# A folded token Fourier transform in a one-core diffusion trunk kernel, with its steps interleaved over four bank sides

## What is computed

```python
def _fourier(f, w_f):
    B, L, _ = f.shape
    fg = f.reshape(B, L, FNET_GROUPS, FNET_GROUP_DIM).astype(jnp.float32)
    z = jnp.fft.fft2(fg, axes=(1, 3), norm='ortho').real.astype(f.dtype)
    return z.reshape(B, L, FNET_DIM) @ w_f
...
y = lax.conv_general_dilated(u, p['conv_w'][:, None, :].astype(u.dtype), window_strides=(1,),
                             padding=((CONV_WIDTH // 2, CONV_WIDTH // 2),),
                             dimension_numbers=('NWC', 'WIO', 'NWC'), feature_group_count=CONV_DIM)
```

## Time and profile before

| | |
|---|---|
| median of 3 runs | 1306.79 us (1306.72 to 1307.79) |
| the profiled execution | 1307.94 us, its span 1306.1 us |
| mean granted TensorE clock | 0.966 of 2.4 GHz |
| busy, PE / DVE / ACT / POOL | 93% / 69% / 47% / 24% of the span |
| Fourier stage on PE, first uv product to first v product | 159.7 to 210.0 us |
| attention on PE | 296.7 to 411.4 us |
| expert stage | from about 740 us on |

### The profile page before, as it was taken

How to read it: one execution, slowest core, us unless ns; L and a number is a source line. 1 busy time by engine, 2 the same in 40 slices (tenths; PEclk the granted TensorE clock), 3 DMA queues, 4 the chain that set the end, 5 groups by cost and what they waited for, 6 DMA issues and landing times.

```text
span 1306.1 us, 18927 instructions
## 1 busy us (share of the span) xinstructions
PE 1215.0 (93%) x7383; PEld 984.0 (75%) x7383; DVE 899.5 (69%) x1015; ACT 617.0 (47%) x686; POOL 311.3 (24%) x207
## 2 busy tenths in 40 slices
PE   4899879998999999999995399999999999999995
PEld 3798669998998999999995266666666666666663
DVE  3599766454553325523747489999999999999996
ACT  4311222224443124123213277777777777777774
POOL 1041100000443222323315202222222222222224
PEclk9899979999999989999997599999999999999998
DMA  9876642322111212244318999999999999999985
GB/s 321 266 205 208 200 93 65 100 78 73 50 50 65 65 33 65 80 162 146 100 44 314 333 346 368 381 379 380 380 379 380 381 381 381 380 381 381 386 312 179
DMA packets 156264, 302.89 MB, mean 232 GB/s; under 512 B 7058, under 2 KB 60821, under 8 KB 155952
## 3 DMA queue, kind: packets, MB, share of 16 engines
q1 hardware_dynamic: 145636, 272.80, 58.4%
q0 software_dynamic: 3872, 12.78, 4.3%
q10 hardware_dynamic: 6700, 16.51, 3.5%
HBM read 286.98 MB, written 15.08 MB: 231 GB/s over the span
## 4 chain that ended last, share of the span: by engine, by line
PE 86%; DVE 5%; DMA 3%; POOL 2%; ACT 1%; issue 1%; SPq 0%; ACTq 0%; POOLq 0%; DVEq 0%
PE bank L1500 17%; PE bank L1501 16%; PE bank L1502 16%; PE bank L1524 5%; PE bank L1526 5%; PE bank L1525 5%; PE bank L1528 5%; PE bank L1529 5%; PE bank L1527 5%; DMA wring<-in_w_ada 2%; PE bank L1752 2%; DVE fa L1060 1%; PE bank L1737 1%; PE bank L1805 1%; PE bank L1924 1%
## 5 line engine op out<-in xcount | busy, mean ns | idle before, releaser
L897 ACT CAST h2r_a<-w_a 128x2048 fp32r<-128x2048 f32 x96 | 183.7, 1914 | 84.8 <-PE bank L1502 77.0
L1500 PE MATMUL bank<-h2r_a,xTh 128*80 128x512 f32 x384 | 152.5, 397 | 1.0 <-DVE xTl L1417 1.0
L563 POOL TENSOR_TENSOR half<-half 1x1 f32<-1x1 f32 x33 | 69.7, 2112 | 351.3 <-DVE ye L1467 348.3
L1502 PE MATMUL bank<-h2r_a,xTl 128*80 128x512 f32 x384 | 150.5, 392 | 0.0
L493 POOL TENSOR_TENSOR lring<-wring,hring 128x2048 fp32r<-128x2048 f32 x21 | 99.1, 4719 | 178.5 <-ACT hring L631 178.5
L1501 PE MATMUL bank<-l2r_b,xTh 128*80 128x512 f32 x320 | 125.8, 393 | 0.0
L1411 DVE TENSOR_TENSOR l2r_b<-w_a,h2r_b 128x2048 fp32r<-128x2048 f32 x48 | 110.3, 2299 | 17.8 <-ACT h2r_b L897 17.8
L1411 DVE TENSOR_TENSOR l2r_b<-w_a,h2r_a 128x2048 fp32r<-128x2048 f32 x48 | 109.9, 2289 | 10.4 <-ACT h2r_a L897 10.4
L1411 DVE TENSOR_TENSOR l2r_a<-w_a,h2r_a 128x2048 fp32r<-128x2048 f32 x48 | 109.5, 2282 | 9.3 <-ACT h2r_a L897 7.7
L1060 DVE SCALAR_TENSOR_TENSOR fa<-fa,cwT 128x655 f32<-128x655 f32 x120 | 111.5, 972 | 1.4
L897 ACT CAST h2r_b<-w_a 128x2048 fp32r<-128x2048 f32 x48 | 91.9, 1914 | 34.7 <-PE bank L1502 31.9
(11 more groups left out here) (344 smaller groups left out, 3036.7 us busy)
## 6 DMA issues: line engine op xcount, KB each, us to landing
w_a<-in_w_e_gate SPq DMA_DIRECT2D x64, 1024.0 KB, 12.2
w_a<-in_w_e_up SPq DMA_DIRECT2D x64, 1024.0 KB, 13.0
w_b<-in_w_e_down SPq DMA_DIRECT2D x48, 1024.0 KB, 12.2
wring<-in_w_in SPq DMA_DIRECT2D x20, 1024.0 KB, 5.3
w_a<-in_w_e_down SPq DMA_DIRECT2D x16, 1024.0 KB, 13.1
fa<-in_w_ada SPq DMA_DIRECT2D x14, 1024.0 KB, 7.8
wring<-in_w_ada SPq DMA_DIRECT2D x10, 1024.0 KB, 9.2
fa<-in_w_in SPq DMA_DIRECT2D x4, 1024.0 KB, 11.2
```

What stands on the lines that cost most here:

```text
L897: act.copy(h2r[k % 3], w2[k]).then_inc(e_hi, 1)
L1500: pe.matmul(out, lh, rh, start=start, stop=False)
L1502: return pe.matmul(out, ll, rh, start=False, stop=stop)
```

## The change

The latent tokens of f are folded: with x the 512 tokens, even part x[t] + x[512 - t] and odd part x[t] - x[512 - t] for t = 1 to 255, and tokens 0 and 256 as they are. The cosine product then needs only the even part, and the sine product only the odd part; and only outputs 0 to 256 are made, from which the others follow by a sum and a difference (`fold_back`). ACT first copies f's latent part to a new tile `fs`, DVE folds it into `eo`, ACT and DVE split `eo`.

- uv(g) has 2 jobs in place of 5: 18 products (3 of 256 columns, 15 of 128, of which 3 for token 256 alone) in place of 15 of 256.
- z(g) has 21 products (9 of 260 columns, 6 of 256, 6 of 128) in place of 24 of 512 and 6 of 128. Of the 9, three are over one partition, for token 256.
- z jobs get bank sides of their own (4 and 5, 6 and 7), and PE's order becomes uv 0, uv 1, z 0, uv 2, z 1, uv 3, z 2, the first value tile, z 3, the other value tiles.
- The tables take one unit (dft 0, three DMAs, 0.5 MB) in place of two of 1 MB; unit in 8 takes the second's place, ahead of the last four ada units.
- `Vs`, from which the values are stored, lies in the tile `vw`. POOL's 8 bias DMAs wait also for ACT's high part of unit in 4.
- Convolution taps: 9 between the f blocks (before 20), 6 in the uv and z steps (18), 7 behind in 9, 6 behind each of in 4, 5, 6, 7, 20, 21, then one in each of the 20 attention iterations that copy an output, and the last 4 at the end of attention.

```diff
-UNITS += [("ada", 18), ("ada", 19), ("dft", 0), ("dft", 1)] + [("ada", i) for i in range(20, 24)]
-UNITS += [("in", i) for i in (8, 9, 4, 5, 6, 7)]
+UNITS += [("ada", 18), ("ada", 19), ("dft", 0), ("in", 8)] + [("ada", i) for i in range(20, 24)]
+UNITS += [("in", i) for i in (9, 4, 5, 6, 7)]
...
+HALF = NS // 2
+DFT_C, DFT_S, DFT_M = 0, 2 * (HALF + 4), 2 * (HALF + 4) + 2 * HALF
+DFT_N = DFT_M + HALF + 4
...
-JOBS += [("uv", 0, t) for t in range(TT)]
-for _g in range(4):
-    if _g < 3:
-        JOBS += [("uv", _g + 1, t) for t in range(TT)]
-    JOBS += [("z", _g)]
-JOBS += [("v", u, t) for u in range(2) for t in range(TT)]
+JOBS += [("uv", g, t) for g in range(2) for t in range(2)] + [("z", 0)]
+JOBS += [("uv", 2, 0), ("uv", 2, 1), ("z", 1), ("uv", 3, 0), ("uv", 3, 1), ("z", 2)]
+JOBS += [("v", 0, 0), ("z", 3)] + [("v", 0, t) for t in range(1, TT)] + [("v", 1, t) for t in range(TT)]
...
+    out, turn = [], 0
+    for j in JOBS:
+        if j == ("fnet", 0):
+            turn = 1
+        if j[0] == "z":
+            out.append(2 + j[1] % 2)
+        elif j[0] == "g2":
+            out.append(0)
+        else:
+            out.append(turn)
+            turn = 1 - turn
+    return out
+
+
+SIDE = sides()
+FIRST, SECOND = (0, 1, 4, 6), (2, 3, 5, 7)
...
-        Vs = xg_f[:, 0:2048].rearrange("p (t d) -> p t d", t=4)
+        Vs = vw[:, :, :, :].rearrange("p a b n -> p (a b) n")
...
+        fs = fa[:, 4608:5632].rearrange("p (b t) -> p b t", b=2)
+        eo = fa[:, 5632:6656].rearrange("p (b t) -> p b t", b=2)
+        qs = xg_f[:, 0:2560].rearrange("p (b t) -> p b t", b=2)[:, :, 1024:1280]
...
+                if UNITS[u][0] == "dft":
+                    x, n = raw(u), HALF + 4
+                    tab = consts["dft_l"]
+                    sp.dma_start(x[:, DFT_C:DFT_S].rearrange("p (c k) -> p c k", c=2), tab[0, :, 0:2, 0:n]).then_inc(s_w[SLOT[u]], 16)
+                    sp.dma_start(x[:, DFT_S:DFT_M].rearrange("p (c k) -> p c k", c=2),
+                                 tab[1, :, 0:2, 0:HALF]).then_inc(s_w[SLOT[u]], 16)
+                    sp.dma_start(x[0:1, DFT_M:DFT_N], tab[0, 0:1, 2, 0:n]).then_inc(s_w[SLOT[u]], 16)
+                    return
...
             gp.wait_ge(s_ada, 24)
+            gp.wait_ge(s_hi, SPLITS.index(U_OF[("in", 4)]) + 1)
             for r in range(8):
...
-                for t, b in job_halves(n):
-                    ins = act.copy(bh[:, i, t], b)
-                ins.then_inc(s_fh, 1)
+                (_, b0), (_, b1) = job_halves(n)
+                act.copy(bh[:, i, 0:NP], b0[:, 0:NP])
+                if i >= 2:
+                    act.wait_ge(s_eo, i - 1)
+                act.copy(fs[:, i % 2, 0:TH - NP], b0[:, NP:TH])
+                act.copy(fs[:, i % 2, TH - NP:NS], b1).then_inc(s_fh, 1)
+                act.wait_ge(s_eo, i + 1)
+                act.copy(bh[:, i, NP:T], eo[:, i % 2, :]).then_inc(s_fh, 1)
...
+                w, n = g % 2, J_OF[("uv", g, 0)]
+                act.wait_ge(s_job, n + 1)
+                act.copy(uvh[:, w, 0:512], bank_a(n)[:, :]).then_inc(s_uvh, 1)
+                n += 1
+                act.wait_ge(s_job, n + 1)
+                act.copy(uvh[:, w, 512:768], bank_a(n)[:, 0:256])
+                act.copy(uvh[0:1, w, 768:896], bank_a(n)[0:1, 256:384]).then_inc(s_uvh, 1)
...
+            def z_out(g):
                 n = J_OF[("z", g)]
                 act.wait_ge(s_job, n + 1)
-                bs, bp = job_bank(n)
-                act.copy(Z[:, g, NP:T], bs)
-                act.copy(Z[:, g, 0:NP], bp).then_inc(s_ja, 1)
-
-            hi(U_OF[("in", 9)])
+                zp, zq = bank_a(n), bank_b(n)
+                act.copy(Z[:, g, 0:NP], zq[:, 0:NP])
+                act.copy(Z[:, g, NP + HALF:NP + HALF + 1], zp[:, HALF:HALF + 1])
+                if g >= 2:
+                    act.wait_ge(s_jd, freed(J_OF[("z", g - 2)])[1])
+                act.copy(qs[:, g % 2, :], zq[:, NP:NP + HALF]).then_inc(s_zq, 1)
...
+            uv_hi(0)
+            uv_hi(1)
+            act.wait_ge(s_rpb2, 16)
+            z_out(0)
+            uv_hi(2)
+            z_out(1)
+            uv_hi(3)
+            z_out(2)
...
+            v_out(0, 0)
+            z_out(3)
+            hi(U_OF[("in", 9)])
+            v_out(0, 1)
+            hi(U_OF[("in", 4)])
...
-                ins.then_inc(s_jd, 1)
+                dve.wait_ge(s_fh, 2 * i + 1)
+                x, y, w = fs[:, i % 2, :], eo[:, i % 2, :], i % 2
+                dve.tensor_tensor(y[:, 1:HALF], x[:, 1:HALF], x[:, NS - 1:HALF:-1], ALU.add)
+                dve.tensor_tensor(y[:, HALF + 1:NS], x[:, 1:HALF], x[:, NS - 1:HALF:-1], ALU.subtract)
+                dve.tensor_copy(y[:, 0:NS:HALF], x[:, 0:NS:HALF]).then_inc(s_eo, 1)
+                dve.tensor_tensor(bl[:, i, 0:NP], bank_a(n)[:, 0:NP], bh[:, i, 0:NP].bitcast(F32), ALU.subtract).then_inc(s_jd, 1)
                 rows_out(16 + 2 * i)
                 ada_mod(15 + 2 * i)
...
-                if i in (1, 2):
-                    lo(U_OF[("dft", i - 1)])
-                conv(4 if i in (1, 2) else 6)
+                if i == 1:
+                    lo(U_OF[("dft", 0)])
+                dve.wait_ge(s_fh, 2 * i + 2)
+                dve.tensor_tensor(bl[:, i, NP:T], y, bh[:, i, NP:T].bitcast(F32), ALU.subtract).then_inc(s_fl, 1)
+                if i == 2:
+                    lo(U_OF[("in", 8)])
+                conv((4, 3, 2, 0)[i])
             ada_mod(23)
-            lo(U_OF[("in", 8)])
 
...
+            def fold_back(g):
+                n = J_OF[("z", g)]
+                dve.wait_ge(s_zq, g + 1)
+                zp, q = bank_a(n), qs[:, g % 2, :]
+                dve.tensor_tensor(Z[:, g, NP:NP + HALF], zp[:, 0:HALF], q, ALU.add)
+                dve.tensor_tensor(Z[:, g, T - 1:NP + HALF:-1], zp[:, 1:HALF], q[:, 1:HALF], ALU.subtract).then_inc(s_jd, 1)
 
             uv_lo(0)
-            for g in range(1, 4):
-                uv_lo(g)
+            uv_lo(1)
+            conv(1)
+            fold_back(0)
+            uv_lo(2)
+            conv(1)
+            fold_back(1)
+            uv_lo(3)
+            fold_back(2)
+            conv(4)
+            fold_back(3)
+            lo(U_OF[("in", 9)])
+            conv(7)
+            for i in (4, 5, 6, 7, 20, 21):
+                lo(U_OF[("in", i)])
                 conv(6)
-
-            for i in (9, 4, 5, 6, 7, 20, 21):
-                lo(U_OF[("in", i)])
-                conv(7)
...
                     dve.tensor_copy(Q[:, hc, x0:x0 + P], bank[3][:, 0:P]).then_inc(s_at, 1)
+                    conv(1)
             conv(CB * CW)
...
+                w, n = g % 2, J_OF[("uv", g, 0)]
+                x = slice(0, P)
+                pe.wait_ge(s_fl, g + 1)
+                bank_free(n)
+                mm3(bank_a(n)[:, 0:256], bh[:, g, 0:P], bl[:, g, 0:P], gtab_h[:, 0:256], gtab_l[:, 0:256], True, True)
+                for j in range(2):
+                    x = slice(NP + j * P, NP + (j + 1) * P)
+                    last = mm3(bank_a(n)[:, 256 + j * P:256 + (j + 1) * P], bh[:, g, x], bl[:, g, x], gtab_h[:, 0:P], gtab_l[:, 0:P],
+                               True, True)
+                last.then_inc(s_job, 1)
+                n += 1
+                bank_free(n)
+                m = slice(NP + HALF, NP + HALF + 1)
+                mm3(bank_a(n)[0:1, 256:384], bh[:, g, m], bl[:, g, m], gtab_h[:, 0:P], gtab_l[:, 0:P], True, True)
+                for j in range(2):
+                    x = slice(NP + HALF + j * P, NP + HALF + (j + 1) * P)
+                    last = mm3(bank_a(n)[:, j * P:(j + 1) * P], bh[:, g, x], bl[:, g, x], gtab_h[:, P:2 * P], gtab_l[:, P:2 * P],
+                               True, True)
+                last.then_inc(s_job, 1)
+
             pe.wait_ge(s_cast, 4)
-            pe.wait_ge(s_turned, 2)
             uv(0)
+            uv(1)
             u = U_OF[("dft", 0)]
-            (ch, cl), (sh, sl) = slot(u), slot(u + 1)
-            for g in range(4):
-                if g < 3:
-                    uv(g + 1)
-                if g == 0:
-                    lo_ready(pe, u + 1)
+            lo_ready(pe, u)
...
+            def z(g):
                 n = J_OF[("z", g)]
-                pe.wait_ge(s_jd, freed(J_OF[("uv", g, TT - 1)])[1])
...
+                w, kn = g % 2, HALF + 4
+                zp, zq, vh, vl = bank_a(n)[:, 0:kn], bank_b(n), uvh[:, w, :], uvl[:, w, :]
+                for j in range(2):
+                    x = slice(256 + j * P, 256 + (j + 1) * P)
+                    mm3(zp, vh[:, x], vl[:, x], table(th, DFT_C, j, kn), table(tl, DFT_C, j, kn), j == 0, False)
+                x, y = slice(768, 896), slice(DFT_M, DFT_N)
+                mm3(zp, vh[0:1, x], vl[0:1, x], th[0:1, y], tl[0:1, y], False, True)
+                for j in range(2):
+                    x = slice(512 + j * P, 512 + (j + 1) * P)
+                    mm3(zq[:, NP:NP + HALF], vh[:, x], vl[:, x], table(th, DFT_S, j, HALF), table(tl, DFT_S, j, HALF), j == 0, j == 1)
```

(37 more changed lines are left out.)

105 lines of the change are left out of this document (39 added, 66 removed).

## The result

The changed kernel takes 1299.93 us (median of 6 runs, 1291.64 to 1300.42) beside 1306.45 (6 runs): a ratio of 0.9938, with a 95% interval of 0.9921 to 0.9956. It is faster by 6.5 us; the forecast was 19.3. The profiled execution took 1300.17 us, its span is 1298.4.

What follows compares the result with a forecast made beforehand. PE was taken to bound the kernel outside the experts (86% of the chain). Terms -30.4 + 2.0 + 3.3 + 1.7 + 3.3 + 0.8 = -19.3 gave 1287.5 us, 8-in-10 range 1279.5 to 1300.

Steps and rivals of the forecast that it cites:

- Clock in the stage: Fourier stage, uv and z products: one short clock fall after the sparse modulation sums, +2.0 us (0 to +17).
- Rival A: Fourier stage: clock stays at 1.2 GHz through uv and z, +11 us, 1298.5 us; chance 17%.
- that landing: Before DVE's last modulation copy: waiting for ACT's earlier store to land, taken as 0, 3 us at the end.
- Rival B: Fourier stage: 8 handover waits of up to 1 us not hidden, or late modulation store, +7, 1294.5 us; chance 12%.
- The folded stage at full clock: uv and z: 18.0 us of products, 1.1 of waits; with f blocks 19.9 for 50.3, -30.4 us.
- The f blocks: DVE's fold work before each modulation row, on PE's path: +0.2 us each, +0.8 in four (0 to +3).
- Attention's start: Before the second scores: 4 more taps, +3.3 us, PE's wait 4.5 us; a clock fall there, +1.7 (0 to +5).
- its end: End of attention: 5 taps before the low part of Z, +3.3 us, wait 5.9; longer low clock, +0.8 (0 to +2).
- inside attention: One tap in each of 20 iterations, hidden in DVE's waits for PE's values: 0 us (to +4).
- Rival C: Attention: DVE's 6.10 us wait before the last split takes the taps, no clock fall; -6, 1281.5 us; chance 13%.
- D: Rival, uv and z: a narrow product costs PE as much as a 512-column one; +18, 1305.5 us; chance 1%.
- E: Rival: wait at attention's start drops the clock and attention's sparse products never restore it; +44, 1331.5 us; chance 4%.

Runs made afterwards that it cites:

- the second trace: The changed kernel, unchanged, run and profiled again as the base of the follow-up runs: 1293.6 us, ratio 0.991 to the kernel before.
- the last row in its own place: Changed kernel with the last modulation row copied to a fifth place, so DVE does not wait for the store before it: 1288.91 us.
- fillers at the sums alone: Changed kernel with extra unused products (2 and 3) only at the two last modulation sums, none before uv(1): 1299.24 us.
- The filled stall: Kernel before the change with 26 unused products in its 6.14 us stall and 5 at the last two modulation sums: 1305.25 us.
- three and four taps: The fastest version with three or four taps moved from behind fold_back(2) to ahead of DVE's split of uv(0): 1290.24 and 1291.68 us.
- the burst of 512-column products: Changed kernel with 18 further unused products of 512 columns behind z(0): 1296.24 us, ratio 0.9916 to the kernel before.
- the fastest version: Changed kernel with the last modulation row in its own place and all taps ahead of attention, no extra products: 1276.25 us.

## Why the prediction was wrong

**The step that failed** is "Clock in the stage": "I take one short fall as at the end of attention ... here +2.0 (0 to +17, the 18 us all at half speed)". The low stretch lasted some 24 us in the profiled execution, which is up to 12 us lost where 2.0 stood; in the second trace it lasted 7, up to 3.5 lost. Measured without the fall, with the last row in its own place, PE took 22.59 us from the first uv product to the second value tile, against 34.29: the fall and the longer wait together cost 11.7. I sized it by the row where products of 320 columns ran for 3.4 us at half clock, and argued that z's products are dense. The rows after the change say that PE can be busy for 100% of 24 us, with products of 128 to 260 columns, and stay at 1.2 GHz. Rival A had the mechanism and the size (+11, 1298.5 us), and I gave it 17%: it was what happened.

**What set it off** I had in hand and priced at nothing: "No row prices that landing; it has a microsecond and a half under uv(0), so 0 is taken, 3 us is the end". The landing took 1.55 us of DVE's time. As waiting that is 0.9 us of PE (1.57 for the 0.7 forecast); as a cause of the fall it is 11 in the executions with the long stretch. The place of the row shows it: 1288.91 without that wait, against the changed kernel's medians of 1299.93 and 1293.6. Rival B named the late store, but not that its price is the clock.

**The other terms held.** The folded stage at full clock: 18.0 us of products and 1.1 of waits. With the row in its own place PE goes from the first uv product at 162.23 to the first value tile at 179.11 and takes 2.78 us more for z(3), together 19.7 us where 19.1 was forecast. No wait on another engine exceeds 0.1 us between z(0) and the value tiles, as forecast. The f blocks +0.8 (0.8). Attention's start +3.2 (3.3), its wait 4.40 (4.5); its end +3.2 (3.3), the wait 5.83 (5.9); the clock +2.0 behind the start (1.7), all of it in the first iteration behind the wait (second to third scores 7.26 us for 5.25); nothing that shows behind the end (0.8); inside attention nothing. Taking the taps out shortened the span from 1298.4 to 1288.6 us, 9.8 for a sum of 3.3 + 1.7 + 3.3 + 0.8 = 9.1, to which the 1.15 us wait of the earlier trace rows belongs, since it went too. With both costs gone the kernel stands at 1276.25, and 1306.79 - 30.4 is 1276.4. That this agrees so closely is partly luck: it also lost that 1.15 us wait, and behind the projection of Z its trace is 1.9 us shorter than that of the kernel before (890.1, 892.1) for no reason that the edits give.

**The early 2.0 us** are not the change's. The first u2 product starts at 37.1 to 37.9 us in some traces and at 39.0 to 39.5 in others, and the changed kernel and the one with fillers at the sums alone, whose programs are the same up to there, stand at 39.24 and 37.64. The same transposes, first in the changed kernel, then in the one with the fillers:

```profile
28.94 1.06 PE L1657 MATMUL bank<-ident,xg_f 128*128 128x128 f32 x4
```

```profile
28.38 0.60 PE L1657 MATMUL bank<-ident,xg_f 128*128 128x128 f32 x4
```

A transpose takes 0.21 us from one start to the next in the first and 0.11 in the second, the steps of 128 columns at the two clocks. Both traces start at the slower step and pass to the faster one, the changed kernel's about 4 us later, though the PEclk column has 1.00 there in both. What sets that moment stays open.

**The stage before.** The filled stall shows that the 0.50 beside the earlier trace rows cost 3.8 us of that stage. The sum did not need this, since it counted the new stage from its products.

Rival C (attention pays less) was wrong: DVE's wait in front of the last split is 6.92 us, but the taps stand behind that split and not ahead of it. D and E did not happen.

## What to carry to other kernels

Before forecasting a stage that becomes dense, ask what PE did in the few microseconds ahead of it. Behind sparse work, a wait of 1.6 us put the next 24 us at half clock and one of 0.8 us did not: 0.8 us of waiting more or less moved the launch by 13.4. A dip of the clock costs most where PE never waits: 24 us at half clock cost over 10 us in the changed kernel, 12.6 us cost 3.8 in the kernel before. So price it from PE's work and waits in the stretch, and not from the PEclk line alone. And an edit meant to lengthen a wait has to be read in the trace first, since work put on an engine that waits anyway costs nothing and tests nothing.

## What the runs showed of the hardware

- At 1.2 GHz products of 128, 256 and 260 columns all step at 0.21 us; at 2.4 GHz at 0.11 and 0.12. The 0.11 us at 128 columns is what the Trainium skill ("TensorE: Matmul & The Clock Gate", LDWEIGHTS (loading the stationary operand)) gives for loading 128 columns of weights. The trace adds the other side: the products for token 256 load one column (163.56, 163.62, 163.68 us in the changed kernel) and step at 0.06 us, at 1.2 GHz at 0.11 (175.12, 175.22, 175.33). So in these rows the step of a product of 128 columns follows the columns of weights that it loads, at either clock, and both kinds take about twice as long at 1.2 GHz.
- A store of 2 KB, issued while the queues carried 1 MB loads at a DMA share of 0.93, took about 4 us to land (159.82 to 163.96, when DVE's wait for it ended).
- The same low stretch ended after 7 us in one execution and after 24 in others, with PE 100% busy in both. The Trainium skill's section "A second HAM failure mode: psum-queue depth-cycling" (same page), in which short idles between groups of products drop the clock again and again, fits the fall. It does not fit the stay: there is no idle time in the stretch. Nor do the 12.6 us of the kernel before, which stood at 0.50 throughout and did not go back and forth, though the prediction calls them in line with it. What lets the stretch end early or late was not found. In all four traces in which it was long (the changed kernel, no taps in attention, three and four taps) the clock came back 1.3 to 4.1 us after PE began the first value tile, 24 products of 256 columns each; whether the one has to do with the other no run tested, and the burst of 512-column products decides little, as said above.
- The same wait does not always bring a fall. PE's wait at the end of attention is 2.64 us in the kernel before and with three and with four taps, and 2.66 in the fastest version; the clock fell behind it in the first two (0.76 over 7 us; 0.72 from 396 to 398 us) and not in the last two (1.00 throughout).
